# Four calls without constant multiplications: the post norms of layers 1 and 2 in a float32 model kernel

## The reference

```
h = rms_norm(x, g_mix_pre);  u = h @ w_in
mix = concat(chunk_attention, conv_module, retention) @ w_out
x = x + rms_norm(mix, g_mix_post)                  # post norm of the mixer
h = rms_norm(x, g_mlp_pre)
f = square(relu(h @ w_up)) @ w_down
x = x + rms_norm(f, g_mlp_post)                    # post norm of the mlp
```

## Time and profile before

| | us |
|---|---|
| median of 3 runs | 2517.69 |
| fastest, slowest of them | 2514.89, 2520.16 |
| the profiled execution: span from first to last instruction | 2514.8 |
| TensorE busy in it | 2475.8 |
| VectorE busy | 1330.1 |
| ScalarE busy | 933.7 |
| GpSimd busy | 277.0 |

### The profile page before, as it was taken

One profiled execution on the slowest core, in us unless ns is written; L12 is line 12 of the kernel. 1 busy time (PEld: TensorE's weight loads), 2 busy tenths in 40 slices (PEclk: granted clock), 3 DMA queues, 4 the chain that ended last, 5 costly groups with the idle time before them and its releaser, 6 DMA issues.

```text
span 2514.8 us, 30384 instructions
## 1 busy us (share of the span) xinstructions
PE 2475.8 (98%) x11796; PEld 1968.6 (78%) x11796; DVE 1330.1 (53%) x1735; ACT 933.7 (37%) x1361; POOL 277.0 (11%) x203
## 2 busy tenths in 40 slices
PE   9999999999999999999999999999999999999998
PEld 7866788887876778888788888877777678888886
DVE  7764642333966463243543437769984476344322
ACT  4344532323434453232332235522235554322321
POOL 1201000001110100000111123300000231111101
PEclk9999999999999999999999999999999999999999
DMA  4401222222230222222222235633342043222232
GB/s 161 147 34 68 84 100 87 97 100 101 76 126 34 84 84 101 96 88 101 84 100 96 88 109 176 214 142 120 132 155 72 26 172 122 101 100 93 76 103 80
DMA packets 46183, 259.54 MB, mean 103 GB/s; under 512 B 5440, under 2 KB 5952, under 8 KB 23168
## 3 DMA queue, kind: packets, MB, share of 16 engines
q1 hardware_dynamic: 44224, 249.47, 28.3%
q0 software_dynamic: 640, 5.51, 0.6%
q10 hardware_dynamic: 1216, 3.15, 0.4%
HBM read 240.27 MB, written 16.78 MB: 102 GB/s over the span
## 4 chain that ended last, share of the span: by engine, by line
PE 89%; DVE 5%; ACT 4%; issue 2%; DMA 0%; POOL 0%; SPq 0%; DVEq 0%; ACTq 0%
PE gemm L445 78%; ACT w_hi L374 1%; PE gemm L657 1%; PE gemm L658 1%; PE gemm L666 1%; DVE x_sb L618 1%; PE score L1805 1%; PE score L869 1%; PE turned L880 1%; DVE w_lo L383 1%; DVE out_sb L554 1%; PE mixed L1815 1%; PE gemm L1912 1%; PE mixed L892 1%; PE turned L1875 1%
## 5 line engine op out<-in xcount | busy, mean ns | idle before, releaser
L383 DVE TENSOR_TENSOR w_lo<-w_raw,w_hi 128x2048 fp32r<-128x2048 f32 (+2 forms) x207 | 439.2, 2122 | 519.8 <-ACT w_hi L374 519.4
L445 PE MATMUL gemm<-h_hi,w_hi 128*128 128x512 f32 x1776 | 704.8, 397 | 0.8 <-ACT u_sb L2067 0.5
L445 PE MATMUL gemm<-h_hi,w_lo 128*128 128x512 f32 x1776 | 692.8, 390 | 0.0
L445 PE MATMUL gemm<-h_lo,w_hi 128*128 128x512 f32 x1776 | 692.0, 390 | 0.0
L374 ACT ACTIVATE w_hi<-w_raw 128x2048 fp32r<-128x2048 f32 (+3 forms) x217 | 381.9, 1760 | 359.8 <-PE gemm L445 327.4
L445 PEld LDWEIGHTS gemm<-h_hi,w_hi 128*128 128x128 f32 x1776 | 335.1, 189 | 81.8 <-issue 10.3
L445 PEld LDWEIGHTS gemm<-h_hi,w_lo 128*128 128x128 f32 x1776 | 333.6, 188 | 71.0
L445 PEld LDWEIGHTS gemm<-h_lo,w_hi 128*128 128x128 f32 x1776 | 334.3, 188 | 66.5 <-issue 1.0
L445 PE MATMUL gemm<-f_hi,w_hi 128*128 128x512 f32 x512 | 199.2, 389 | 0.0
L445 PE MATMUL gemm<-f_lo,w_hi 128*128 128x512 f32 x512 | 199.2, 389 | 0.0
L445 PE MATMUL gemm<-f_hi,w_lo 128*128 128x512 f32 x512 | 199.2, 389 | 0.0
(11 more groups left out here) (416 smaller groups left out, 3473.7 us busy)
## 6 DMA issues: line engine op xcount, KB each, us to landing
w_raw<-in_w SPq DMA_DIRECT2D x171, 1024.0 KB, 4.7
w_raw<-in_w SPq DMA_DIRECT2D x16, 768.0 KB, 4.0
w_raw<-in_w SPq DMA_DIRECT2D x16, 640.0 KB, 3.7
w_raw<-in_w SPq DMA_DIRECT2D x18, 512.0 KB, 3.5
trig_kept<-made SPq DMA_DIRECT2D x16, 512.0 KB, 5.8
trig<-trig_kept SPq DMA_DIRECT2D x16, 512.0 KB, 6.4
bias_t<-in_att_bias SPq DMA_DIRECT2D x2, 1536.0 KB, 9.5
decay_t<-in_c_decay SPq DMA_DIRECT2D x2, 1536.0 KB, 8.8
```

The costliest lines, as they stand in the source:

```text
L383: dve.tensor_tensor(w_lo[:, b.slot, 0:size], w_raw[:, b.slot, 0:size], w_hi[:, b.slot, 0:size].bitcast(F32), ALU.subtract).then_inc(S["w_r ...
L445: mm = pe.matmul(dst, lhs, rhs, start=b.first and k == 0 and j == 0, stop=b.last and k == b.kt - 1 and j == 2)
```

## The change

The calls of `keep_clock` behind the two `added_total` of `layer_tensor` are taken out. `layer_tensor` is built for two layers, so this is four places of four calls each. The call in `begin_tensor` stays, and no other engine's order is touched.

```diff
             added_total(pe, N0 + 1, sq_f)
-            keep_clock(pe, t_ps[:, 0:416], ones[:], fixed[:, 0:416], 4)
             for half in range(2):
                 first = plan1[UP[half]]
...
             added_total(pe, N0 + 3, sq_f)
-            keep_clock(pe, t_ps[:, 0:384], ones[:], fixed[:, 0:384], 4)
```

## The result

The changed kernel takes 2521.81 us (median of 21 runs, 2520.19 to 2522.95) against 2517.69 us before (21 runs, 2514.89 to 2520.16): ratio 1.0017, 95% interval 1.001 to 1.0023. That is 4.1 us or 0.17% more: the interval doesn't contain 1, but the size is within the 0.2% to which the forecast gave 0.61. The profiled execution has a span of 2519.5 us, 4.7 us more than before's. One reading of mine is to be mended: an execution's own time is 1.8 us above its span in every run where both are listed (2521.34 with 2519.5), so the profiled execution of before took about 2516.6 us, and that the fastest run shown looked equal to its span was chance.

The account below looks back on a forecast made before the run. TensorE, busy for 98% of the span, was taken to bound the kernel. 0 saved and 4 x 1.05 = 4.2 us lost to clock falls, on the median 2517.7, gave 2521.9 us; range 2517 to 2526.5.

Parts of the forecast that it names:

- the 0.2% to which the forecast gave 0.61: Whole kernel: time within 0.2% (5.0 us) of before, chance 0.61; slower by more 0.36, faster by more 0.03.
- The removal saves nothing: At the four places: constants lie inside TensorE's wait on the 3.60 us chain L540 to L575, so the saving is 0.
- The rival that the constants slow this chain: L540 to L575: PSUM contention from the constants, 0.4 us gained over four places, 2517.3 us; chance 0.03.
- The clock falls at each place: All four bare places: TensorE idle 3.65 to 3.73 us, then clock at 0.50 for about 3.4 us.
- 1.59 us for a stretch inside the opening, 0.56 us of it caught: Each opening: 3.41 us at half clock loses 1.59 us; slack from DVE and ACT pacing absorbs 0.56, leaving 1.0 us.
- The long stretch: Rival at all four places: clock stays down twice as long, 10.4 us lost, 2528.1 us; chance 0.14.
- my upper bound: One place: stretch bounded by twice the seen one, 6.8 us, a loss of 3.2 - 0.56 = 2.6 us.
- 1.05 us for each place: Middle value taken for one fall at each of four places, with early falls and long stretches pulling opposite ways.
- The early, cheap falls of 0.2 us: Clock falls 1.7 us ahead of L657, so part of the stretch is idle: loss 0.8 - 0.56 = 0.2 us.
- a sign that I had given for being wrong: Changed profile: clock down for about 6.8 us at several places would mean 2526 us or more.
- All of it reaches the end: Behind the openings: work follows TensorE's own products, so what the slack leaves of each loss goes through to the end.
- 4.2 us on the median: Whole kernel: 4 x 1.05 = 4.2 us put on the median 2517.7, giving 2521.9 us, 0.17% more.

Follow-up runs that it names:

- the inner calls: Kernel before with all constants, plus one or two calls of 512 columns inside each of the four openings; with two: 2521.89 against 2517.07 us, ratio 1.0024.
- two late calls: Kernel before with two calls of constants instead of four at each place, issued only after ACT's first half of the root: 2517.52 against 2516.60 us, ratio 1.0003.

## Why the prediction was right

- *The removal saves nothing:* so it was. L575 ends 3.60 us after L540 starts with and without the constants (3.51 us at the mlp places), and L657 follows it by 0.10 us. The rival that the constants slow this chain is out.
- *The clock falls at each place:* all ten bare places in three profiles fell (twice four, and the two mixer places), and none of the 26 places with four calls did, in seven profiles. Of the moment I had said late in the idle time to a few tenths of a microsecond into the opening; it was 1.98 us ahead of the opening to 1.17 us into it.
- *1.59 us for a stretch inside the opening, 0.56 us of it caught:* 1.00 to 1.01 us measured at the short falls of the first profile, and the slack by itself was measured as 0.55 to 0.58 us with the inner calls. By the Trainium skill's rule ("TensorE: Matmul & The Clock Gate", Part 1: throttled time times one half) it would have been 1.71 - 0.56 = 1.15 us; the ratio of the rows was nearer, since the 0.230 us between products at full clock are more than half of the 0.43 us at half clock.
- *The long stretch:* I gave it 0.14 as a case at all four places. It is neither rare nor general: one of four and two of four places in the two profiles. It costs 1.7 to 2.0 us, not the 2.6 of my upper bound, because 1.4 to 2.0 us of it lie in the idle time. That is the one term mis-sized: 1.05 us for each place was 1.18 in the first profile and 1.41 in the second (4.71 / 4 and 5.63 / 4). The early, cheap falls of 0.2 us, which were to balance it, were not seen at a bare place: all four falls that came early stayed long. So the middle value that I took for each place had a wrong reason, though it was near. The second profile also shows a sign that I had given for being wrong, about 6.8 us at half clock at several places (two), and yet took 2522.8 us and not the 2526 that I had put beside it.
- *All of it reaches the end:* shown by 4.71 us of places in 4.7 us of span, and by the inner calls.
- *4.2 us on the median:* measured 4.1, and the match to 0.1 us is luck. The profiles show 4.7 and 5.6 us from the places, and before's own scatter of 5.3 us (against 2.8 after) may lift its median. What stands behind that scatter is open in part. In the 50 executions of before that ran beside the experiments, the 41 with a mean granted clock of 0.998 took 2514.80 to 2518.23 us and the nine with 0.997 or 0.996 took 2517.95 to 2519.84 us, so there are executions with more time at half clock; neither profile of before is one of them. In the 21 executions of the two versions that hold the clock in the third layer, none was below 0.998. This points there, but doesn't show it.

## What to carry to other kernels

Work that nobody reads can pay for itself, where the engine that bounds the kernel waits on a chain that it doesn't feed and its granted clock falls in or behind the wait. Here it is worth 4 to 6 us of 2518. To judge such a filler, don't look at its busy time or at the 40 slices: look at the granted clock in windows of a few microseconds behind the gap, at the spacing of equal products there, and at how much slack the next stage has before it feels the loss. Price one fall, count the places, and expect a whole that is near the scatter of the runs; the distance between two landmarks in the profile tells 0.1 us where the time of a run can't tell 2 us.

## What the runs showed that I had not expected

- The clock does not fall at a fixed length of idle time. Over all profiles, an idle time of 3.65 to 3.73 us cost it at 10 of 10 places, 3.0 us at 2 of 4, 2.31 us in the third layer in 9 of 10 profiles and 2.33 to 2.36 us ahead of an opening at 2 of 4, and 1.9 us at about 2036 us in 2 of 11. A place can hold in one execution and fall in the next.
- Every fall that ended within the kernel lasted one of two lengths, 3.41 or 6.83 us. The four long ones are those that began 1.4 to 2.0 us ahead of the opening with TensorE idle until then. The one that began 2.1 us ahead of it and was short, with two late calls, had constants to multiply from its start on. That the work makes the difference is read from these few falls and was not tested.
- The clock can fall while TensorE is busy: 1.2 us after the opening's start (268.85 against 267.69), as well as before it.
